# A wide product over the input's high and low parts in the expert-value stage of a Trainium2 kernel, with the halves added by VectorE

## What is computed

```python
def _peer(hn, w_query, sub_keys, expert_down, expert_up):
    q = (hn @ w_query).reshape(b, s, PEER_HEADS, 2, PEER_QUERY_DIM // 2)
    sc = jnp.einsum('bshcd,hckd->bshck', q, sub_keys).astype(F32)
    v1, i1 = lax.top_k(sc[..., 0, :], PEER_TOPK)
    v2, i2 = lax.top_k(sc[..., 1, :], PEER_TOPK)
    ...
    top, pos = lax.top_k(cand, PEER_TOPK)
    idx = jnp.take_along_axis(cidx, pos, axis=-1)
    gate = jax.nn.softmax(top, axis=-1)
    ...
        u = expert_down[ib]
        act = jax.nn.gelu(jnp.einsum('bld,blhkd->blhk', hb, u), approximate=False)
        coef = (gb * act.astype(F32)).astype(hb.dtype)
        vv = expert_up[ib]
        return jnp.einsum('blhk,blhkd->bld', coef, vv)
```

## Time and profile before

| what | us |
|---|---|
| time before, median of 3 runs | 3827.81 (3827.61 to 3828.02) |
| the profiled execution | 3826.34 |
| its span in the profile | 3824.5 |
| TensorE busy in the span | 3495.3 |
| VectorE busy | 2522.5 |
| ScalarE busy | 1893.9 |
| DMA queue of the loads, share of 16 engines | 54.1% |

### The profile page before, as it was taken

The page is one execution under the profiler, slowest core; times in us unless marked ns, Lnnn a source line. Parts: engine busy times, 40 slices in busy tenths (PEclk is TensorE's granted clock), DMA queues, the critical chain, the costliest instruction groups (busy, mean ns, idle before and its releaser), DMA issues. The chain is left out here.

```text
span 3824.5 us, 54885 instructions
## 1 busy us (share of the span) xinstructions
PE 3495.3 (91%) x21873; PEld 3087.6 (81%) x21873; DVE 2522.5 (66%) x3058; ACT 1893.9 (50%) x2033; POOL 55.7 (1%) x35
## 2 busy tenths in 40 slices
PE   4999889989887799999999996898787999999999
PEld 4988779989787578777877776798477999977887
DVE  5767455478555388888888873353653788495665
ACT  2533433354433467676767652353343444474554
POOL 0000000000000000000000000000000000000000
PEclk9999989989998899999999998899898999999999
DMA  6740346368012399999999972353033455504554
GB/s 225 246 151 1 111 181 232 139 204 303 6 67 82 109 361 367 359 363 360 368 360 363 359 280 99 111 177 132 7 110 111 154 181 181 182 7 135 194 193 159
DMA packets 296869, 739.08 MB, mean 193 GB/s; under 512 B 17449, under 2 KB 17904, under 8 KB 291312
## 3 DMA queue, kind: packets, MB, share of 16 engines
q1 hardware_dynamic: 296688, 736.60, 54.1%
HBM read 735.50 MB, written 1.05 MB: 193 GB/s over the span
## 5 line engine op out<-in xcount | busy, mean ns | idle before, releaser
L2068 DVE TENSOR_TENSOR weight_ring_low<-weight_ring,weights_high 128x2048 fp32r<-128x2048 f32 x336 | 773.6, 2344 | 148.7 <-ACT weights_high L2014 148.7
L2014 ACT ACTIVATE weights_high<-weight_ring 128x2048 fp32r<-128x2048 f32 x336 | 618.3, 1907 | 6.2 <-DMA weight_ring<-in_moe_w 6.2
L378 PE MATMUL psum_all<-h_high_projections,high_projections 128*128 128x256 f32 x1536 | 440.0, 286 | 25.5 <-DVE h_low_projections L313 25.4
L378 PE MATMUL psum_all<-h_low_projections,high_projections 128*128 128x256 f32 x1536 | 436.4, 284 | 0.0
L378 PE MATMUL psum_all<-h_high_projections,weight_ring_low 128*128 128x256 f32 x1536 | 431.1, 281 | 0.0
L1956 PE MATMUL psum_all<-weights_high,expert_in_turn_high 128*128 128x512 f32 x896 | 359.1, 401 | 18.1 <-DVE weight_ring_low L2068 11.9
L1956 PE MATMUL psum_all<-weights_high,expert_in_turn_low 128*128 128x512 f32 x896 | 356.3, 398 | 0.0
L1956 PE MATMUL psum_all<-weight_ring_low,expert_in_turn_high 128*128 128x512 f32 x896 | 351.6, 392 | 0.0
L378 PEld LDWEIGHTS psum_all<-h_high_projections,high_projections 128*128 128x128 f32 x1536 | 291.6, 190 | 30.1 <-DVE h_low_projections L313 30.1
L378 PEld LDWEIGHTS psum_all<-h_high_projections,weight_ring_low 128*128 128x128 f32 x1536 | 296.4, 193 | 0.0
L433 DVE TENSOR_TENSOR weight_ring_low<-weight_ring,high_projections 128x2048 fp32r<-128x2048 f32 x96 | 215.8, 2287 | 121.6 <-ACT high_projections L391 121.6
(11 more groups left out here) (612 smaller groups left out, 7909.6 us busy)
## 6 DMA issues: line engine op xcount, KB each, us to landing
weight_ring<-in_moe_w SPq DMA_DIRECT2D x336, 1024.0 KB, 5.1
weight_ring<-in_w_in SPq DMA_DIRECT2D x48, 2048.0 KB, 8.6
expert_rows<-in_peer_down SPq DMA_DIRECT2D x128, 512.0 KB, 3.2
expert_rows<-in_peer_up SPq DMA_DIRECT2D x128, 512.0 KB, 3.2
weight_ring<-in_ffn_halves SPq DMA_DIRECT2D x42, 1024.0 KB, 6.0
branch_out<-in_ada_w SPq DMA_DIRECT2D x64, 512.0 KB, 9.9
weight_ring<-in_w_out SPq DMA_DIRECT2D x6, 2048.0 KB, 8.4
weight_ring<-in_ada_w SPq DMA_DIRECT2D x4, 2048.0 KB, 11.5
```

The lines of the kernel that those rows point to most:

```text
L378: mm = pe.matmul(half(k.ps, 4 * (g % R) + j), w[:, c, j * P:(j + 1) * P], x[:, c], start=(c == 0 and n == 0), stop=(c == KC - 1 and n == 2))
L2014: act.activation(high[:, q, h * HALF:(h + 1) * HALF], k.ring[:, q, h * HALF:(h + 1) * HALF], ACT.Copy).then_inc(high_made[q], 1)
L2068: dve.tensor_tensor(k.low[:, q, part], k.ring[:, q, part], high[:, q, part].bitcast(F32), ALU.subtract).then_inc(low_made[q], 1)
```

## The change

The input's high and low parts are laid into one tensor `m.h_both` (two blocks in the free dimension, at the addresses that they had before). For each of the eight feature blocks TensorE now makes two matmuls where it made three: weights high by both input parts, 512 columns, which fill the whole bank (columns 0 to 255 by the high part, 256 to 511 by the low part), and weights low by input high, 256 columns, into the first half. The two halves of the bank have to be added afterwards. ScalarE copies the second half into the grid (`copied`), VectorE adds the first half out of PSUM to it (`join`, counted by `joined`), and ScalarE takes the Gelu in place, grid to grid. A bank is free for unit n + 3 when unit n is joined.

The order by hand changes with it. On ScalarE, the copy of unit n stands ahead of the high part of unit n + 3, and the Gelu of unit n, behind that high part, waits for the join. On VectorE, the join of unit n stands ahead of the low part of unit n + 3. `norm` moves from unit 76 to unit 78. The last three joins stand behind the last low part.

```diff
--- before.py
+++ after.py
@@ -2876,8 +2876,9 @@
         self.raw = units("expert_rows", 0, PEER_RAW, F32)
         self.low = units("expert_rows_low", 0, PEER_RAW, F32R)
         self.high = units("expert_rows_high", PEER_RAW, PEER_HIGH, F32R)
-        self.h_high = units("peer_h_high", PEER_RAW + PEER_HIGH, 2, F32R, [P, KC, T])
-        self.h_low = k.nc.alloc_sbuf_tensor_at("peer_h_low", [P, KC, T], F32R, offset=k.h_at)
+        high_at = k.ring_at + (PEER_RAW + PEER_HIGH) * 4096
+        self.h_both = k.nc.alloc_sbuf_tensor_at("peer_h_both", [P, 2, (k.h_at - high_at) // 4], F32R, offset=high_at)
+        self.h_high, self.h_low = (self.h_both[:, n, 0:KC * T].rearrange("p (c t) -> p c t", c=KC) for n in range(2))
         self.first = units("peer_first", PEER_RAW, 2, F32, [P, 4, QUAD, NK])
         self.second = units("peer_second", PEER_RAW + 2, 2, F32, [P, 4, QUAD, NK])
         self.apart = units("peer_apart", PEER_RAW + 4, 2, F32, [P, 4, QUAD * NK])
@@ -2978,7 +2979,7 @@
     SCORES_END, LATE = 96 - 16, 104
     with k.stage("peer_values") as st:
         block = st.block
-        high_made, low_made, summed, gelued, chain, ranked, apart, exped, normed, chosen, turned, moved = st.signals(12)
+        high_made, low_made, summed, copied, joined, gelued, chain, ranked, apart, exped, normed, chosen, turned, moved = st.signals(14)
 
         @block.gpsimd
         def _(pool):
@@ -2993,11 +2994,11 @@
         def product(pe, s, it):
             n = it * PEER_RAW + s
             pe.wait_ge(low_made, n + 1)
-            pe.wait_ge(gelued, n + 1)
+            pe.wait_ge(joined, n + 1)
             for c in range(KC):
                 hi, lo = m.high[:, s % PEER_HIGH, c * P:(c + 1) * P], m.low[:, s, c * P:(c + 1) * P]
-                for q, (w, x) in enumerate(((hi, m.h_high), (hi, m.h_low), (lo, m.h_high))):
-                    mm = pe.matmul(half(k.ps, 2 * (s % 3)), w, x[:, c], start=(c == 0 and q == 0), stop=(c == KC - 1 and q == 2))
+                pe.matmul(k.ps[:, s % 3, :], hi, m.h_both[:, :, c * T:(c + 1) * T], start=(c == 0), stop=False, skip_group_check=True)
+                mm = pe.matmul(k.ps[:, s % 3, 0:T], lo, m.h_high[:, c], start=False, stop=(c == KC - 1), skip_group_check=True)
             mm.then_inc(summed, 1)
 
         @block.tensor
@@ -3015,8 +3016,6 @@
 
         @block.scalar
         def _(act):
-            act.sem_inc(gelued, 3)
-
             def high(n):
                 act.wait_ge(k.experts_in[n % PEER_RAW], loaded_units(n))
                 act.activation(m.high[:, n % PEER_HIGH], m.raw[:, n % PEER_RAW], ACT.Copy).then_inc(high_made, 1)
@@ -3032,9 +3031,11 @@
                     act.activation(m.lists[:, 1], half(k.ps, 10), ACT.Copy).then_inc(moved, 1)
                     act.activation(m.i2_minus[:], half(k.ps, 9), ACT.Copy, scale=-1.0).then_inc(moved, 1)
                 act.wait_ge(summed, n + 1)
+                act.activation(m.grid[:, n:n + 1], k.ps[:, n % 3, T:2 * T].unsqueeze(1), ACT.Copy).then_inc(copied, 1)
                 if n + PEER_HIGH < NK:
                     high(n + PEER_HIGH)
-                act.activation(m.grid[:, n:n + 1], half(k.ps, 2 * (n % 3)).unsqueeze(1), ACT.Gelu).then_inc(gelued, 1)
+                act.wait_ge(joined, n + 4)
+                act.activation(m.grid[:, n:n + 1], m.grid[:, n:n + 1], ACT.Gelu).then_inc(gelued, 1)
                 if n == EXP_AT:
                     act.wait_ge(apart, 1)
                     act.activation(top[:], top[:], ACT.Exp).then_inc(exped, 1)
@@ -3047,6 +3048,11 @@
                 dve.wait_ge(high_made, n + 1)
                 dve.tensor_tensor(m.low[:, n % PEER_RAW], m.raw[:, n % PEER_RAW], m.high[:, n % PEER_HIGH].bitcast(F32),
                                   ALU.subtract).then_inc(low_made, 1)
+
+            def join(n):
+
+                dve.wait_ge(copied, n + 1)
+                dve.tensor_tensor(m.grid[:, n], m.grid[:, n], k.ps[:, n % 3, 0:T], ALU.add).then_inc(joined, 1)
 
             def top16(src, vals, idx):
                 link(dve.max(vals[:, 0:8], src))
@@ -3099,7 +3105,10 @@
                 side, i = divmod(n, TT)
                 dve.tensor_reduce(key[:, side, i].rearrange("p h r -> p (h r)"), f, AX.X, ALU.add).then_inc(chosen, 1)
 
+            dve.sem_inc(joined, 3)
             for n in range(NK):
+                if n >= PEER_HIGH:
+                    join(n - PEER_HIGH)
                 low(n)
                 if n < 40 and n % 5 < 4:
                     rows(n // 5 * 4 + n % 5)
@@ -3112,7 +3121,7 @@
                     lift()
                 if n == 74:
                     places()
-                if n == EXP_AT + 2:
+                if n == EXP_AT + PEER_HIGH + 1:
                     norm()
                 if 77 <= n < 101:
                     if (n - 77) % 6 == 0:
@@ -3121,6 +3130,8 @@
                         take((n - 77) // 6)
                     if (n - 77) % 6 == 4:
                         gather((n - 77) // 6)
+            for n in range(NK - PEER_HIGH, NK):
+                join(n)
 
 
 def peer_grid(k, m):
```

## The result

The changed kernel takes 3835.32 us, the median of 21 runs (3832.76 to 3837.46), beside 3828.14 us before (21 runs). By the medians it is 7.2 us longer. A second measurement, beside the experiments, gave 3835.34 us and 1.0017 (1.0008 to 1.0026). The prediction was 3833.3 us, 5.5 over before, most likely no difference that counts.

The account below looks back on a forecast made before the run. TensorE was taken as the bound before, VectorE in 72 units after the change. Terms 5.5 + 7.8 - 6.0 - 2.9 + 0.8 = +5.2 us on the 3827.81 us median, plus 0.3, gave 3833.3 us; range 3822 to 3845.

Parts of the forecast that it names:

- the ring: Chain join, Gelu, copy, high part, low part: 2.15 us, so VectorE stands 0.33 us in units without side work (short units).
- TensorE's part: Eight wide and eight narrow products a unit: 2.773 us instead of 2.88, saving 0.107 us where TensorE stays the bound.
- light units: The 56 units outside 0 to 39 and 41 to 72, where TensorE's pitch counts: 56 x -0.107 = -6.0 us.
- The join on VectorE: Adding the bank's halves costs VectorE 0.34 us to the next start, against 0.26 to 0.27 spare a unit in 72 units.
- (b): Rival: join, Gelu and copy cost their drained time (join 0.46 us), +9.6 on the forecast, 3842.9 us; chance 0.20.
- The stretches: Units with rankings, where VectorE becomes the bound: +5.5 us in units 0 to 39, +7.8 in units 41 to 72.
- the lead: VectorE enters heavy stretches ahead, with time used up before TensorE stands; gives back 0 to 5.8 us, taken as 2.9.
- The end of the stage: After the last product come copy, join and Gelu instead of one Gelu: +0.8 us.
- late first products: Short waits of TensorE's first product in a unit that it has stood before: 0.3 us added, an estimate.
- (a): Rival: the join fits into VectorE's idle time, so TensorE's saving stays, -13.7 + 0.8, 3814.9 us; chance 0.07.
- (c): Rival: the wide product saves little (operand in two pieces or small fixed cost), 2.86 us a unit, 3838.2 us; chance 0.13.
- (d): Rival: TensorE's clock falls to 1.2 GHz because it stands some 0.25 us in 72 units, 3970 us; chance 0.02.

Follow-up runs that it names:

- e3_gelu_later: The changed kernel with each Gelu moved one unit later on ScalarE, behind the next copy and high part: 3827.63 us, ratio 0.9996 to the kernel before.
- e1: The changed kernel without copy and join, wide products kept, Gelu reading only the bank's first half (sum incomplete): 3817.88 us, ratio 0.9972 to the kernel before.
- e2: The changed kernel with narrow products again, 24 a unit, but copy, join and in-place Gelu kept: 3837.98 us, ratio 1.0025 to the kernel before.
- e10: e1 with the input's two parts side by side, so a wide product's 512 columns are one address run: 3818.48 us, ratio 0.9977 to the kernel before.
- e4: The change in units 72 to 127 only, units 0 to 71 as in the kernel before: 3825.3 us, ratio 0.9994 to the kernel before.
- e5: e4 with four of each six of the first 72 units wide too and the Gelu one unit later: 3822.8 us, ratio 0.9988 to the kernel before.
- e8: e5 with each unit's low-part products placed behind all its high-part ones: 3821.5 us, ratio 0.9981 to the kernel before.
- e11: e5 with the input's two parts side by side in one row of addresses: 3823.09 us, ratio 0.9990 to the kernel before.
- e7: e1 with each unit's eight wide products first and its eight narrow ones after, instead of alternating: 3819.43 us, ratio 0.9976 to the kernel before.

## Why the prediction was right

The forecast, that VectorE becomes the bound in 72 units and the ring adds to it, holds step by step.

- **TensorE's part**: 2.773 us a unit where it is the bound, to the third place. It holds for one of the two pitches, from unit 72 on in the first trace and from 102 on in the second. At the other (2.828) the gain is 0.052 a unit, half. For the 56 light units the sum had 6.0 us; behind unit 72 the first trace shows 6.4 (84.08 and 75.52 against 80.43 and 72.77; 0.6 of it is a stop of TensorE near the exponential that the kernel before had) and the second 4.9. The sum had no term for that stop, nor for the slower pitch.
- **The join on VectorE**: taken at 0.34 to the next start, 0.33 by the timeline. This was the choice that decided between the forecast and rival (b), and the unlinked step of the earlier trace rows was the right row to go by.
- **The ring**: 2.12 us instead of 2.15, and 0.32 us lost in a short unit instead of 0.33. e3_gelu_later gives back 7.6 us, where the sum had 24 x 0.33 = 7.9. It was worked out from the order of the instructions and the durations of single ones, and it is shown.
- **The stretches**: +5.5 and +7.8 less the lead of 2.9 is +10.4; measured +4.1 and +6.6, that is +10.7. The lead was taken in the middle between 0 and 5.8. What is left over for it by the table is 2.6 (5.5 + 7.8 - 10.7), but no run measures it by itself.
- **The end of the stage**: +0.8 in the sum. Before, the last Gelu ended 0.42 us after the last product (3346.60 and 3346.18), now 1.32 us after it (3354.38 and 3353.06), +0.9. The first trace has the stage at +5.2 us, the sum at +5.2. That they agree to a tenth is luck: the heavy stretches lost 0.3 more than forecast, the end 0.1 more, and the light units gained 0.4 more, and the second trace, at the slower pitch in 29 units, has +6.8. The 0.3 us added for late first products is shown by no run.
- **Rivals**: (a), with the joins at no cost, falls with the time itself and with e1 and e2, which part the gain of the wide products from the cost of the joins. (b), drained steps, falls with the timeline. (c), a wide product that saves little, came true in part: at the slower pitch a unit saves 0.052 us, half of the 0.107. Its reason doesn't hold for that pitch, since e10 has it with the operand in one row. (d), the clock, falls: it is 1.00 from 2990 us to the end of the stage, and lower only in the first units, behind a pause (0.64 from 2976 to 2980 us; 0.77 before). The Trainium skill's sentence on clock swings from short idle times ("TensorE: Matmul & The Clock Gate", section "A second HAM failure mode: psum-queue depth-cycling") does not come true here: in the first 72 units the first product of 32 came 0.1 to 0.7 us late, at a granted clock of 1.00 from 2990 us on. The Trainium skill's isolated gap of N / 2.4 + 2.5 ns (same page, section "Back-to-back issue gap") would by an estimate have given the wide product a gain of 2.6 us, and e1 shows 11.7 in the stage.

Measured were 7.2 us by the medians, 5.5 were predicted, and 5.5 is inside the interval. The slower pitch in the light units (1.6 us in the second trace) may have a part in the difference, but it isn't shown: the run of the first trace took 3835.61 us and that of the second, with the longer stage, 3832.35.

## What to carry to other kernels

An idle total (94 us of VectorE's) doesn't say whether work fits; the spare time in each stretch does, and here it was 0.26 us a unit in 72 of 128 units, against a join of 0.34. When an instruction gets a new wait, look at what stands behind it in its queue and whether the waited-for engine needs that: moving the waiting Gelu one unit back gave back what the ring had cost (7.6 us in the heavy units), with no instruction less. And a saving of TensorE time pays only where TensorE is the bound, so it can be switched on by stretch (e4, e5, e8) rather than everywhere.

## What the runs showed of the hardware

- A stream that alternates a 512-column and a 256-column product has two steady paces: 0.3467 us and 0.3535 us a pair. In the nine traces with such a stream the pace changes 72 times between two units that follow one another. Each time TensorE had stood in between (0.08 us or more) or run something else, as the transposes at unit 102. Over 863 borders without a stop it never changed, and over 60 with one it stayed as it was. What decides between the two isn't known, and nothing tried here chose one of them. In the units behind 72 it made the stage of the changed kernel 1.6 us longer in one trace than in the other; all 56 at the slower pace would make it 3.1 (an estimate, 56 x 0.055).
- Streams of 256 columns alone ran at 0.120 us in every trace that has them (the kernel before, e2, e4, e5, e8, e11).
- With the wide and narrow products of a unit grouped (e7, e8), one pace was seen: 0.230 us a wide product, 0.120 a narrow one.
- In a stream without waits the fixed cost of a product over its columns at 2.4 GHz is about 13 ns for 256 columns and, in the last stage and at the faster pace, for 512. So one wide product in place of two narrow ones saves about 13 ns, 0.107 us for the eight in a unit. At the slower pace it saves about half of that, and grouped about 10 ns.
